# The last gate tile of a streaming-encoder trunk on one NeuronCore: 24 + 6 products of 256 tokens, or twice as many of 128

## What is computed

```
D_MODEL, SEQ, DEPTH, PLE_DIM = 1024, 256, 2, 256
for i in range(DEPTH):
    x = x + 0.5 * swiglu(rmsnorm(x, norm_ff1[i]), ...)
    x = x + token_mixer(rmsnorm(x, norm_mix[i]), ...)
    x = x + 0.5 * swiglu(rmsnorm(x, norm_ff2[i]), ...)
    g = jax.nn.sigmoid(rmsnorm(x, norm_ple[i]) @ ple_w_gate[i])     # the gates
    x = x + g * (p[i] @ ple_w_proj[i])                              # the projection
return rmsnorm(x, norm_final)
```

## Time and profile before

| | |
|---|---|
| Time, median of 3 runs (lowest to highest) | 1175.71 us (1175.65 to 1175.8) |
| The profiled execution: its time / its span | 1175.59 us / 1173.7 us |
| TensorE busy / weight loads busy | 99% / 97% |
| VectorE / ScalarE / GpSimd busy | 70% / 52% / 10% |
| Chain of work that ended last | TensorE 98%, DMA 1%, VectorE 1% |
| Mean granted TensorE clock | 0.998 |

### The profile page before, as it was taken

How to read it: one execution, slowest core, us unless ns; L and a number is a source line. 1 busy time by engine, 2 the same in 40 slices (tenths; PEclk the granted TensorE clock), 3 DMA queues, 4 the chain that set the end, 5 groups by cost and what they waited for, 6 DMA issues and landing times.

```text
span 1173.7 us, 24027 instructions
## 1 busy us (share of the span) xinstructions
PE 1166.6 (99%) x10518; PEld 1142.9 (97%) x10518; DVE 820.7 (70%) x936; ACT 609.7 (52%) x688; POOL 117.1 (10%) x130
## 2 busy tenths in 40 slices
PE   9999999999999999999999999999999999999998
PEld 9999999999999999999999999999899999999998
DVE  6866545697978766655786665458799787666556
ACT  6544445555745644444764443446466555444445
POOL 2000001011512000001110000100134020000011
PEclk9999999999999999999999999999999999999999
DMA  8655555545445555555556555554644456555551
GB/s 294 232 202 190 189 206 169 193 150 200 154 145 194 200 193 201 192 187 198 191 175 224 183 203 189 183 214 140 220 145 146 143 204 211 205 182 202 192 180 37
DMA packets 33528, 218.87 MB, mean 186 GB/s; under 512 B 5200, under 2 KB 6544, under 8 KB 7440
## 3 DMA queue, kind: packets, MB, share of 16 engines
q1 hardware_dynamic: 32992, 216.82, 53.3%
q10 hardware_dynamic: 432, 0.52, 0.1%
HBM read 216.15 MB, written 1.05 MB: 185 GB/s over the span
## 4 chain that ended last, share of the span: by engine, by line
PE 98%; DMA 1%; DVE 1%; ACT 0%; SPq 0%; issue 0%; DVEq 0%
PE psum L409 32%; PE psum L410 31%; PE psum L411 31%; PE psum L691 1%; PE psum L670 1%; DMA x_all<-in_x 1%; PE psum L543 0%; PE psum L604 0%; PE psum L654 0%; PE psum L725 0%; DVE gates L1801 0%; PE psum L736 0%; PE psum L639 0%; PE psum L759 0%; DVE hB_lo L1769 0%; PE psum L586 0%
## 5 line engine op out<-in xcount | busy, mean ns | idle before, releaser
L1309 DVE TENSOR_TENSOR w_lo<-raw,w_hi 128x2048 fp32r<-128x2048 f32 x200 | 457.9, 2292 | 218.2 <-ACT w_hi L905 218.0
L905 ACT ACTIVATE w_hi<-raw 128x2048 fp32r<-128x2048 f32 x201 | 385.2, 1916 | 352.3 <-PE psum L411 347.7
L409 PE MATMUL psum<-hA_hi,w_hi 128*128 128x256 f32 x1360 | 377.6, 278 | 0.0
L410 PE MATMUL psum<-hA_hi,w_lo 128*128 128x256 f32 x1360 | 375.7, 276 | 0.0
L411 PE MATMUL psum<-hA_lo,w_hi 128*128 128x256 f32 x1360 | 375.7, 276 | 0.0
L409 PEld LDWEIGHTS psum<-hA_hi,w_hi 128*128 128x128 f32 x1360 | 255.4, 188 | 2.7 <-issue 2.7
L410 PEld LDWEIGHTS psum<-hA_hi,w_lo 128*128 128x128 f32 x1360 | 255.4, 188 | 0.0
L411 PEld LDWEIGHTS psum<-hA_lo,w_hi 128*128 128x128 f32 x1360 | 255.3, 188 | 0.0
L409 PE MATMUL psum<-hB_hi,w_hi 128*128 128x256 f32 x832 | 229.9, 276 | 0.6 <-DVE w_lo L1777 0.6
L410 PE MATMUL psum<-hB_hi,w_lo 128*128 128x256 f32 x832 | 229.7, 276 | 0.0
L411 PE MATMUL psum<-hB_lo,w_hi 128*128 128x256 f32 x832 | 229.7, 276 | 0.0
(11 more groups left out here) (207 smaller groups left out, 1241.4 us busy)
## 6 DMA issues: line engine op xcount, KB each, us to landing
raw<-in_weights SPq DMA_DIRECT2D x203, 1024.0 KB, 4.9
raw<-in_weights SPq DMA_DIRECT2D x2, 512.0 KB, 6.3
x_all<-in_x SPq DMA_DIRECT2D x1, 520.0 KB, 3.6
x_all<-in_x SPq DMA_DIRECT2D x1, 512.0 KB, 6.3
relu<-in_p SPq DMA_DIRECT2D x2, 256.0 KB, 5.1
consts<-in_consts SPq DMA_DIRECT2D x1, 384.0 KB, 5.1
out<-gates ACTq DMA_DIRECT2D x2, 192.0 KB, 2.3
out<-gates SPq DMA_DIRECT2D x2, 192.0 KB, 2.3
```

Source lines behind the costliest of these rows:

```text
L409: pe.matmul(o, lh, rh, start=start, stop=False)
L410: pe.matmul(o, ll, rh, start=False, stop=False)
L905: act.activation(w_hi[:, s, :], raw[:, s, :], ACT.Copy).then_inc(hi_ready[s], 1)
L1309: dve.tensor_tensor(w_lo[:, s, :], raw[:, s, :], w_hi[:, s, :].bitcast(F32), ALU.subtract).then_inc(lo_ready[s], 1)
```

## The change

Only the last tile of the last layer changes. Its products are taken for tokens 0 to 127 first (24 for the gates, then 6 for the projection) and then again for tokens 128 to 255. Each has 128 streamed columns and loads its own 128x128 weights, as before. The gates of the halves lie in banks 6 and 7, the projections in banks 0 and 1. Each half signals for itself (`gate_half`, `last_projected`), and VectorE waits for each. TensorE's waits for the projection weights, for an update of x (now the second of the embedding step and not the first, since bank 1 is used too) and for the third scaling (bank 6) stand ahead of the tile. The warming product in bank 6 gets a wait for the first half's scaling.

```
-                        pairs(s, LAST_TILES[1] - 1, hA, 1, range(8)).then_inc(chunk_done[s], 1)
                         if L == L_N - 1:
-                            pe.wait_ge(last_weights_lo, 1)
-                            pe.wait_ge(x_done, L * 16 + 13)
-                            for k in range(2):
-                                mm = three(bank[0][:, 0:T], last_w_hi[:, k, :], last_w_lo[:, k, :], pT_hi_[:, k, :], pT_lo_[:, k, :],
-                                           k == 0, k == 1)
-                            mm.then_inc(last_projected, 1)
+                            last_tile(s)
+                        else:
+                            pairs(s, LAST_TILES[1] - 1, hA, 1, range(8)).then_inc(chunk_done[s], 1)
+
+            def last_tile(s):
+
+                wh, wl = (w[:, s, :].rearrange("p (k n) -> p k n", n=256) for w in (w_hi, w_lo))
+                pe.wait_ge(last_weights_lo, 1)
+                pe.wait_ge(x_done, (L_N - 1) * 16 + 14)
+                pe.wait_ge(pgate_scaled, L_N * 4 - 1)
+                for t in range(2):
+                    tokens = HALVES[t]
+                    for k in range(8):
+                        mm = three(bank[HALF_BANKS[t]][:, tokens], wh[:, k, P:2 * P], wl[:, k, P:2 * P],
+                                   hA[0][:, k, tokens], hA[1][:, k, tokens], k == 0, k == 7)
+                    mm.then_inc(gate_half, 1)
+                    for k in range(2):
+                        mm = three(bank[PROJECTED_BANKS[t]][:, tokens], last_w_hi[:, k, :], last_w_lo[:, k, :],
+                                   pT_hi_[:, k, tokens], pT_lo_[:, k, tokens], k == 0, k == 1)
+                    mm.then_inc(last_projected, 1)
...
-            pe.wait_ge(pgate_scaled, L_N * 4 - 1)
...
+            pe.wait_ge(half_scaled, 1)
             keep_warm(WARM_BEFORE_SUMS)
...
-                    chunk_products(L, PGATE + 3)
                     for t in range(2):
-                        dve.tensor_tensor(gate_sum[:, 1, HALVES[t]], bank[LAST_TILES[1]][:, HALVES[t]], rb[:, HALVES[t]], ALU.mult
+                        dve.wait_ge(gate_half, t + 1)
+                        dve.tensor_tensor(gate_sum[:, 1, HALVES[t]], bank[HALF_BANKS[t]][:, HALVES[t]], rb[:, HALVES[t]], ALU.mult
                                           ).then_inc(half_scaled, 1)
-                    dve.wait_ge(last_projected, 1)
                     for t in range(2):
+                        dve.wait_ge(last_projected, t + 1)
                         dve.wait_ge(half_tanh, t + 1)
```

More of the change, by code:

```diff
@@ L31 @@
 LAST_TILES = (5, 7)
+HALF_BANKS = (6, 7)
+PROJECTED_BANKS = (0, 1)
 UP_BANKS = (6, 7, 0, 1, 2, 3)
@@ L267, in hybrid_trunk @@
         last_projected = sem("last_projected")
+        gate_half = sem("gate_half")
         half_scaled = sem("half_scaled")
@@ L1704, in last_tile @@
                 def last_tile():
-                    chunk_products(L, PGATE + 3)
                     for t in range(2):
-                        dve.tensor_tensor(gate_sum[:, 1, HALVES[t]], bank[LAST_TILES[1]][:, HALVES[t]], rb[:, HALVES[t]], ALU.mult
+                        dve.wait_ge(gate_half, t + 1)
+                        dve.tensor_tensor(gate_sum[:, 1, HALVES[t]], bank[HALF_BANKS[t]][:, HALVES[t]], rb[:, HALVES[t]], ALU.mult
                                           ).then_inc(half_scaled, 1)
-                    dve.wait_ge(last_projected, 1)
                     for t in range(2):
+                        dve.wait_ge(last_projected, t + 1)
                         dve.wait_ge(half_tanh, t + 1)
                         g = gate_act[:, 1, HALVES[t]]
-                        dve.scalar_tensor_tensor(out=g, in0=g, scalar=1.0, in1=bank[0][:, HALVES[t]], op0=ALU.add, op1=ALU.mult
+                        dve.scalar_tensor_tensor(out=g, in0=g, scalar=1.0, in1=bank[PROJECTED_BANKS[t]][:, HALVES[t]], op0=ALU.add, op1=ALU.mult
                                                  ).then_inc(half_gated, 1)
```

## The result

| | Before | Changed |
|---|---|---|
| Time, median of 10 runs (lowest to highest) | 1175.8 us (1175.65 to 1176.04) | 1178.89 us (1178.6 to 1179.62) |
| Ratio, 95% interval | | 1.0028 (1.0020 to 1.0036) |
| Span of the profiled execution | 1173.7 us | 1176.8 us |
| TensorE busy / matmuls in the trace | 1166.6 us / 10518 | 1169.1 us / 10548 |

The changed kernel is 3.1 us slower; 1178.9 was forecast. The trace has 30 matmuls more and TensorE is busy 2.5 us longer. Seven of its ten runs took 1178.6 to 1178.97 us and list a mean granted clock of 0.998; the other three (1179.08, 1179.56, 1179.62 us) list 0.997, and as none of the three was profiled, it stays open where their clock was lower.

What follows compares the result with a forecast made beforehand. TensorE, busy 99%, was taken as the bound: its last tile grows from 3.44 to 6.86 us, later steps move by 3.2 to 3.42, taken as +3.3 on 1175.59, giving 1178.9 us; range 1176.8 to 1181.0 us.

Steps and rivals of the forecast that it cites:

- The slot: Last tile on TensorE: a 128-column gate product starts every 0.113 us, set by its weight load; chance 0.67.
- The bounds taken with it: Limits for a last-tile product: 0.057 us by stream alone, 0.227 us if it costs what plain fp32 does.
- The projection's slot: Last tile's 12 projection products on TensorE: kept at 0.12 us each.
- The gating: VectorE, second half: projection last by a hair, gating starts at 1168.76 instead of 1165.59 us, 3.17 us later.
- The sums: Behind the last tile: TensorE's 1.29 us of work now binds the first sum, moving it by 3.42 us.
- The total: Whole kernel: profiled execution of 1175.59 us plus 3.3 us gives 1178.9 us.
- The moved waits and the banks: TensorE's waits moved ahead of the last tile cost nothing; separate banks remove no stall the trace shows.
- A (stream): Last tile: streamed columns set the slot, 0.057 us, so no change at 1175.7 us; chance 0.07.
- B (something between): Last tile: loads run faster behind short streams, 0.085 us per product, 1177.3 us; chance 0.09.
- C (as plain fp32): Last tile: products under 256 columns run as plain fp32, 0.227 us each, 1185.8 us; chance 0.11.
- D (0.14): Last tile: load and stream overlap less well, 0.14 us per product, 1180.6 us; chance 0.06.
- denser work can't slow the clock: TensorE in the last tile: clock granted in full up to 1165 us, 0.96 on average after; no slowing expected.

Runs made afterwards that it cites:

- the first experiment: Changed kernel with each of the last tile's 60 products streaming all 256 tokens instead of 128; 1178.98 us, ratio 1.0028 to the kernel before.

## Why the prediction was right

**The slot.** This was the step on which the sign hung, and it was right for the reason given: the weight load sets it. The row that said so was the earlier trace rows, a stretch where next to nothing is streamed and where the loads stand alone. 0.113 was used and 0.112 measured. The bounds taken with it held as well: with half the weights the slot fell to 0.060, against 0.057 for the stream alone, and plain fp32 took 0.225 against 0.227. One sentence went too far, that no row shows such loads closer than 0.11 us. The kernel before has transposes (line 654) with loads of 128x128:

```profile
282.26 0.20 PEld L654 LDWEIGHTS psum<-consts,prob 128*128 128x128 f32 x2 [0.17 <-issue]
...
894.55 0.60 PE L654 MATMUL psum<-consts,prob 128*128 128x128 f32 x4
```

The two loads of the first row are 0.14 us long each, so they start 0.06 apart. The second row is a stream again: four products of 128 columns, each 0.28 us long and behind a load of its own, so (0.60 - 0.28) / 3 = 0.11 us apart. It bears on the slot as the warming products do, though its load records are shorter than the 0.19 us of a gate product.

**The projection's slot** was sized wrong. 0.12 us was kept from the earlier trace rows where 0.112 was measured. With 256 streamed columns it is again (1168.36 - 1168.00) / 3 = 0.12 in the first experiment, and 0.111 with 192. So 0.12 was never the load: it belongs to products of 256 streamed columns. I carried a stream's number into a place where the load binds. Why it is more than the gates' 0.113 is open; in the first experiment the gate products right behind the first projection take 0.12 too. Over 12 products that is 0.1 us too much. The gates' 0.001 us each add 0.06, and the first slot of the tile, 0.06 in place of 0.11, the rest: the tile came out at 6.65 us and not 6.86.

**The gating.** Forecast at 1168.76, measured 1168.72, but by errors that cancel, and the step that was said to be last is not. The prediction lets scaling follow the gates by 0.15 us and gating follow the projection by 0.17, each 0.05 less than before for a stream half as long. No run shows this saving. Scaling still comes 0.20 us behind the gates (1167.98 against 1167.78), and the one gating that waited for nothing but a halved projection, the second of the run with the projection halved, also comes 0.20 behind it (1166.04 against 1165.84). By that the projection, whose slots end at 1168.45, would have let the gating start at 1168.65. It starts at 1168.72, and that is 0.10 us behind the end of tanh, the same 0.10 as at the first gating of that run (tanh from 1165.08 to 1165.39, gating at 1165.49). The label in brackets names PE, but the chain that ended last goes by tanh (start us, us, what):

```profile
1167.83 0.13 PE psum L414
1167.98 0.30 DVE gates L1724
1168.31 0.32 ACT gates L1164
1168.72 0.29 DVE gates L1730
```

So the late half's gates, scaling and tanh set the time, and the projection behind them had 0.07 us to spare. In the kernel before the two ways are only 0.02 us apart: tanh 1164.98 + 0.31 + 0.10 = 1165.39, the projection 1165.17 + 0.20 = 1165.37. That the projection was last there, as the prediction read it, is not shown either. TensorE's end came 0.14 us earlier than forecast (1168.45 against 1168.59), the steps behind it took more, and that the forecast of 1168.76 is only 0.04 off is in part luck.

**The sums.** I took the 1.29 us between 1165.17 and 1166.46 as TensorE's own work and concluded that it would now bind the first sum and move it by 3.42. That was wrong. The changed kernel needs 1169.62 - 1168.45 = 1.17 us for the same products: before, the last 0.1 us had been a wait for the first square (which ended at 1166.40). In both kernels the square of half 0 is what the first root hangs on. Before:

```profile
1166.11 0.29 DVE L1722 SCALAR_TENSOR_TENSOR relu<-x_all 128x128 f32<-128x128 f32 x1
1166.45 0.30 PEld L870 LDWEIGHTS psum<-ones_r,relu 128*128 128x128 f32 x2
```

Changed:

```profile
1169.59 0.30 PEld L885 LDWEIGHTS psum<-ones_r,relu 128*128 128x128 f32 x2
1170.01 0.26 ACT L1179 ACTIVATE mean<-psum,half_neg 128x1 f32<-128x1 f32 x1
```

The load of the first sum starts 0.05 or 0.06 us behind the end of that square (1166.40 and 1166.45; 1169.53 and 1169.59), and the root 0.48 behind it (1166.88 in the earlier trace rows; 1170.01). The run with the projection halved has the same distance within 0.01 (1166.86 and 1167.33), and there the table load ended 0.44 us ahead of the root, so it isn't the table load that sets it. The squares moved by 3.13 us with the gating (1169.24 against 1166.11), and so did the roots and the final multiplies. This is why the shift was 3.13 and not the 3.3 that I took from between the two paths.

**The total.** 1178.9 was forecast and 1178.89 measured. That the two agree so closely is luck: the sum started from a profiled execution of 1175.59 us, 0.2 below the median of 1175.8, and added 3.3 where the timelines show 3.13.

**The moved waits and the banks** cost nothing: the first product of the tile starts 0.11 us behind the one ahead of it (1161.80 and 1161.69), so TensorE did not stand at the waits. Nor did the banks bring a gain that any run shows.

**The rivals.** A (stream) and B (something between) fell with the slot. The Trainium skill, "TensorE: Matmul & The Clock Gate", "Back-to-back issue gap", has about 81 ns for a load and matmul pair at 128 columns; this case measures 112 with full fp32 weights of 128 columns and 60 with 64 of them, and the measurement decides. C (as plain fp32) is excluded, its price confirmed at 1185.42 us. D (0.14) did not occur: the slot is 0.112, the distance of the loads, so load and stream overlap.

What I had not seen at all is that such a split touches the clock. With 128 columns the trace shows it at full level through the tile; with 96 and 64 it fell. The prediction's sentence that denser work can't slow the clock there was a right result on a wrong footing, and that it came out right was luck: the work was not denser but thinner, half the columns in the same time.

## What to carry to other kernels

In these runs a product's slot is the larger of what it streams and what it loads. Where the two are nearly equal, as here at 256 columns and 128x128 fp32 weights, splitting the streamed side only multiplies the loads. To learn the price of the load, look for a stretch of the trace where almost nothing is streamed and read the starts of the weight loads. And before half of a tile is made early, look for who would use it: here VectorE had the late half's first step queued ahead, and with that changed, the sums behind all products and a table load of ScalarE took back the gain. Last, a label that names what ended a wait is not proof where two things end within 0.1 us: compare the distances with a row in which only one of them can have been last.

## What the runs showed of the hardware

- With weights of 128 columns of fp32 loaded for each product, the slot is 0.111 us at the 2.4 GHz level for 64 to 192 streamed columns, and 0.213 us at 1.2 GHz; with weights of 64 columns it is 0.060 us.
- TensorE lost half its clock in the middle of gapless work when 64 or 96 columns were streamed in each 0.111 us slot, and kept it with 128 in the profiled execution. In the run with 64 in the first half only, it fell about 1 us after that half was over, when 128 were streamed again. A stretch that is bound by weight loads can cost twice: once in slots, and again in the clock (1181.8 to 1183.0 us for less work than the changed kernel's 1178.9).
- A longer stretch than the 6.65 us with 128 columns was not tried in the rounded format. The plain fp32 run has matmul records of 128 columns, one each 0.11 us, from 1161.88 to 1175.27 us, and kept its clock throughout:

```profile
1172.00:1174.00 2.00, 2.00 (x20) 2.00 (x20) 0.00 (x0) 0.00 (x0) 0.00 (x0) 1.00 0.00 0
```
